# Rotary rotation moved from a product on TensorE to DMAs between partitions, with the index rope four attention units later

## The chip, the cores and the metric

One core of one Trainium2 chip runs the whole program as one launch. The metric is the device time of that launch in microseconds (us). Engines: TensorE (PE, with its weight loads as PEld), VectorE (DVE), ScalarE (ACT), GpSimd (POOL), and SyncE (SP), which issues the weight loads. Each engine works through its own list of instructions in order; semaphores tie the lists together.

## The reference, cut to what matters

A first block (a convolution mixer and a mixture of 32 experts) is followed by two layers of a second block. Only the second block is touched:

```python
def apply_rope(x, cos, sin):
    x1, x2 = jnp.split(x, 2, axis=-1)               # halves of a head's 64 channels
    return jnp.concatenate([x1 * c - x2 * s, x2 * c + x1 * s], axis=-1)

for l in range(DEPTH_2):                             # two layers
    (qa, ka, va, qb, kb, vb, qc, kc, vc, qi, ki, wi, gates) = split(rmsnorm(x) @ w_in[l])
    o_a = chunk_band_attention(qa, ka, va, rel_bias_a[l])
    o_b = diff_attention(apply_rope(qb), apply_rope(kb), vb, lam, lam_init, subln_b[l])
    o_c = dsa_attention(apply_rope(qc), apply_rope(kc), vc, apply_rope(qi), apply_rope(ki), wi, topk)
    ...                                              # gates, up, out, cross attention, swiglu
```

Everything is float32. Five tensors a layer go through `apply_rope`: qb, kb, the index pair (qi and ki together, called idx), qc and kc.

## The kernel before

Activations lie transposed: 128 channels on the partitions (two heads of 64), 256 tokens along a row. A tensor of heads is `[128, 4, 256]`, four blocks of 128 channels; idx has three blocks. A weight of 1024 x 128 is a "chunk". For each chunk ACT writes a rounded copy `w_hi` ("split", line 1292), DVE writes the rest `w_lo` ("low", line 529), and PE multiplies three times (lines 734, 735, 737). For the chunks of qc, kc and vc (35 to 46 of a layer) POOL does the low part, on the same line 529. Four chunk buffers (`PARTS`) go round, so ACT may split chunk n+4 only when PE has used chunk n.

The order of a layer is the hand-written list `WORK` (line 157); `with_splits` puts the splits and lows into it, and every engine walks through the result. `attention(first, last, extra)` lays out the attention units: at step s come "probs" of unit s-1, the extra work of the step, "scores" of unit s, "turn" (transposes) of unit s-1 and "apply" of unit s-2. Units 0 to 7 are attention A, with one chunk of gate projections as extra work at steps 1 to 8. At each unit DVE adds the bias and takes the row maximum (1730, 1731), ACT takes the exponential (1179), DVE divides by the sum (1737, 1745), PE transposes (1045), ACT copies the transposed probabilities out (`probsT`), PE applies them (1064), and ACT copies the result out (`outs`, which frees the unit's PSUM).

PSUM is four "duos" of 1024 columns. `seat` gives every tenant a duo and a turn: units go round duos 0 to 2, gate tenants g_0 to g_5 take duo 3, all others go round all four. `enter` waits until the tenant before in the same duo has been freed. Unit 5 sits where unit 2 sat.

A rope is: PE multiplies the heads by a constant matrix `rotate` of +1 and -1, which swaps the 32-partition halves of each head with a sign (line 996); DVE multiplies that product by `sin_r` (1698); POOL multiplies the heads by `cos_r` in place (1857); DVE adds the two (1703). The ropes of qb and kb stand behind the projections of kb and vb. The index rope stands at step 1 of attention A, behind "probs" 0. With it go the index weights: PE turns 64 rows of `score` into PSUM (1000), and DVE scales them into `wi` (1709), which frees the tenant p_idx. p_idx sits in duo 1 and the next tenant there is unit 1; g_0 follows vb in duo 3.

After attention A comes the index stage: two top-64 selections on DVE ("index" 0 and 1; products on line 1755, eight values at a time on 1760 and 1762, the selection on 1763), while PE runs the projections of qc, kc and vc and their two ropes. After it DVE does the rope of qc, the lows of chunks 47 to 49, the rope of kc and the scores of unit 8, in this order.

Of the kernel before, what the change touches and what calls it, by code (L numbers as in the profile page):

```python
# [13 lines left out]
ALU = mybir.AluOpType  # L14
# [30 lines left out]
LAYER_LINKS = 124  # L45
# [106 lines left out]
def gate_parts(starts, piece, gate):  # L152
# [7 lines left out]
        + attention(0, 8, {**gate_parts((1, 5), 7, 0), 1: [("rope", 2, "idx"), ("gates", 7, 0, 0)]})  # L160
# [74 lines left out]
def tenants(work):  # L235
    names = []
    for w in work:
# [5 lines left out]
        elif kind == "rope":  # L243
            names.append(f"r_{w[2]}")
# [43 lines left out]
def build(nc, x, mem, cst, vec1, vec2, relpad, w_in, w_out, w1, w3, w2, w_in_2, w_up_a, w_up_b, w_up_c,  # L288
# [11 lines left out]
    with ExitStack() as ctx:  # L300
        def sb(name, shape, dt=F32):
            return ctx.enter_context(nc.sbuf_tensor(name, shape, dt))
# [47 lines left out]
        rtok = sb("rtok", [P, 16])  # L350

# [69 lines left out]
        def small(*dims):  # L421
# [34 lines left out]
         lam_dot, lam_exp, rot_done, cos_ready, rope_ready, idx_raw, wi_turned, idx_done, relu_ready, selneg_ready,  # L456
# [10 lines left out]
            "lam_dot lam_exp rot_done cos_ready rope_ready idx_raw wi_turned idx_done relu_ready selneg_ready "  # L467
# [29 lines left out]
        def arrived(eng, i):  # L497
            eng.wait_ge(ring_full[MIX_SLOTS[i]], MIX_SLOTS[:i + 1].count(MIX_SLOTS[i]) * 16)

# [196 lines left out]
        def _(pe):  # L696
# [261 lines left out]
            for l in range(LAYERS):  # L958
                for w in WORK:
# [27 lines left out]
                    elif kind == "rope":  # L987
                        r, name = w[1], w[2]
                        if name == "idx":
                            pe.wait_ge(idx_raw, l + 1)  # L990
                        else:
                            freed(pe, f"p_{name}", l)
# [5 lines left out]
                        if name == "idx":  # L998
                            for t in range(TT):
                                last = pe.transpose(duo("p_idx")[:, 768 + 64 * t:832 + 64 * t],  # L1000
                                                    score[64:128, t * P:(t + 1) * P], ident[64:128, 64:128])
                            last.then_inc(wi_turned, 1)
# [172 lines left out]
        def _(act_e):  # L1175
# [107 lines left out]
            for l in range(LAYERS):  # L1283
                for w in WORK_SPLIT:
# [29 lines left out]
                    elif kind == "proj" and w[2] not in ("qa", "ka"):  # L1314
                        product_done(act_e, w[1], l)
                        name = w[2]
                        copy(heads[name], view(duo(f"p_{name}"), 0, 4, SEQ)).then_inc(free_of(f"p_{name}"), 1)
                    elif kind == "proj_v":
# [7 lines left out]
                    elif kind == "index_proj":  # L1326
# [4 lines left out]
                        copy(score[64:128, :], duo("p_idx")[64:128, 512:768]).then_inc(idx_raw, 1)  # L1331
                    elif kind == "gates":
# [69 lines left out]
        def _(v):  # L1402
# [29 lines left out]
            v.wait_ge(consts_in, 32)  # L1432
            norm("n_mix", 1, xT, g1("norm_mix"), hT)
# [202 lines left out]
            for l in range(LAYERS):  # L1636
                link, linked = linker(v, layer_chain, LAYER_LINKS, l)
                for w in WORK_SPLIT:
# [23 lines left out]
                    elif kind == "root":  # L1662
# [31 lines left out]
                    elif kind == "rope":  # L1694
                        r, name = w[1], w[2]
                        k = 3 if name == "idx" else 4
                        v.wait_ge(rot_done, l * 5 + r + 1)
# [8 lines left out]
                        if name == "idx":  # L1706
# [233 lines left out]
```

## Time and profile before

| | |
|---|---|
| time, median of 3 runs | 1865.93 us (1864.66 to 1867.06) |
| the profiled execution | 1867.45 us, its span 1865.7 us, so 1.75 us lie around the span |
| PE busy | 1673.9 us, 90% |
| DVE / ACT / POOL busy | 881.0 / 586.0 / 95.4 us |
| mean granted PE clock | 0.951 |
| first block, then two layers | layers from about 694 us to 1274 us and from there to 1851 us |

The trace gives for each instruction its start, its length, and, where its engine stood idle before it, how long and which instruction released it. A length contains time in which the instruction waited inside its engine. The second layer repeats the first 576.5 us later, to within a few hundredths of a us in the stretches used here (ACT's table load behind the idx copies starts at 787.85 and at 1364.35 us), so every reading is made in the first and counted twice.

### The profile page before, as it was taken

Reading aid. Unit: us, or ns where it says so; the run is one execution under the profiler, and the core shown is the slowest. Engines: PE = TensorE matmul, PEld = TensorE weight load, DVE = VectorE, ACT = ScalarE, POOL = GpSimd, SP = SyncE. Lnnn points to the kernel's source line nnn. Section 1 sums busy time; section 2 is a strip of 40 time slices with the busy share of each in tenths; the row PEclk is TensorE's granted clock in tenths of the full one; section 3 lists DMA queues with packets and bytes.
Section 4 is the critical chain, followed back from the end, with each engine's and each line's share of the span. In section 5 each row is a group of like instructions: output and inputs, shape, how many; then the busy total and the mean of one; then the engine's idle time right before and its main releaser. Section 6 shows DMA issues by size and latency. Waiting matters only on the chain.

```text
span 1865.7 us, 24506 instructions
## 1 busy us (share of the span) xinstructions
PE 1673.9 (90%) x10574; PEld 1335.2 (72%) x10574; DVE 881.0 (47%) x1157; ACT 586.0 (31%) x881; POOL 95.4 (5%) x50
## 2 busy tenths in 40 slices
PE   6948799999999969998999799998999799889997
PEld 5836544344443438877779689998978678779997
DVE  1782311111011136568745376646467755366653
ACT  1030211111111124453532344434454451244442
POOL 0000000000000000134000000000016000000000
PEclk8978799999999999999999799999999999979998
DMA  9052199999999974423323255473434224326550
GB/s 341 1 225 90 70 428 430 429 428 428 429 430 427 428 284 145 160 101 126 136 88 138 90 181 181 166 244 136 163 120 158 91 91 142 128 91 199 175 192 23
DMA packets 121739, 388.73 MB, mean 208 GB/s; under 512 B 3504, under 2 KB 55088, under 8 KB 109360
## 3 DMA queue, kind: packets, MB, share of 16 engines
q1 hardware_dynamic: 121648, 387.40, 54.1%
q8 instruction: 71, 1.16, 0.3%
q14 instruction: 20, 0.16, 0.0%
HBM read 386.34 MB, written 1.05 MB: 208 GB/s over the span
## 4 chain that ended last, share of the span: by engine, by line
PE 63%; DVE 17%; DMA 10%; ACT 6%; issue 2%; SPq 0%; DVEq 0%; ACTq 0%
DMA ring<-w 10%; PE psum L915 9%; PE psum L734 7%; PE psum L735 7%; PE psum L737 7%; PE psum L1092 4%; PE psum L724 4%; PE psum L937 3%; DVE outs L1452 3%; PE psum L766 3%; PE psum L1151 2%; PE psum L1154 2%; PE psum L1153 2%; ACT probs L1179 2%; DVE w_lo L529 2%
## 5 line engine op out<-in xcount | busy, mean ns | idle before, releaser
L529 DVE TENSOR_TENSOR w_lo<-raw,w_hi 128x1024 fp32r<-128x1024 f32 x250 | 305.8, 1240 | 196.0 <-ACT w_hi L1182 195.0
L1182 ACT ACTIVATE w_hi<-raw 128x1024 fp32r<-128x1024 f32 x274 | 284.4, 1053 | 282.8 <-PE psum L737 111.2
L734 PE MATMUL psum<-h_hi,w_hi 128*128 128x256 f32 x1456 | 364.2, 288 | 8.5 <-DVE big L1680 6.8
L735 PE MATMUL psum<-h_hi,w_lo 128*128 128x256 f32 x1456 | 358.8, 284 | 0.0
L734 PEld LDWEIGHTS psum<-h_hi,w_hi 128*128 128x128 f32 x1456 | 280.7, 193 | 14.9 <-DVE big L1680 8.5
L735 PEld LDWEIGHTS psum<-h_hi,w_lo 128*128 128x128 f32 x1456 | 280.8, 193 | 0.1
L915 PE MATMUL psum<-ring,outs 128*64 128x512 f32 x1024 | 231.5, 608 | 23.9 <-DMA ring<-w 22.5
L915 PEld LDWEIGHTS psum<-ring,outs 128*64 128x64 f32 x1024 | 81.3, 140 | 172.0 <-issue 172.0
L737 PE MATMUL psum<-h_lo,w_hi 128*128 128x256 f32 x1456 | 204.2, 283 | 0.0
L1613 DVE TENSOR_TENSOR qk<-big,psum 128x512 f32<-128x512 f32 x16 | 17.2, 1077 | 368.3 <-PE psum L915 368.3
L737 PEld LDWEIGHTS psum<-h_lo,w_hi 128*128 128x128 f32 x1456 | 187.8, 192 | 0.0
L1182 ACT ACTIVATE qk<-psum 128x1024 f32<-128x1024 f32 (+1 forms) x48 | 39.6, 829 | 343.1 <-PE psum L922 166.1
L937 PE MATMUL psum<-ring,qk 128*64 128x512 f32 x512 | 113.4, 595 | 0.0
L1151 PE MATMUL psum<-act_parts,w_hi 128*128 128x256 f32 x352 | 98.9, 281 | 0.0
L1153 PE MATMUL psum<-act_parts,w_hi 128*128 128x256 f32 x352 | 98.9, 281 | 0.0
L1154 PE MATMUL psum<-act_parts,w_lo 128*128 128x256 f32 x352 | 98.9, 281 | 0.0
L1179 ACT ACTIVATE probs<-probs,stat 128x256 f32<-128x256 f32 (+1 forms) x112 | 50.8, 454 | 123.3 <-DVE stat L1731 123.3
L1092 PE MATMUL psum<-outs,raw 128*128 128x256 f32 x384 | 83.2, 379 | 0.0
L937 PEld LDWEIGHTS psum<-ring,qk 128*64 128x64 f32 x512 | 35.3, 137 | 66.8 <-issue 66.8
L1857 POOL TENSOR_TENSOR qk<-qk,std 128x1024 f32<-128x1024 f32 x8 | 21.1, 2635 | 1189.2 <-PE psum L996 1189.2
L1092 PEld LDWEIGHTS psum<-outs,raw 128*128 128x128 f32 x384 | 73.0, 190 | 10.0
L724 PE MATMUL psum<-hT,ring 128*128 128x256 f32 x320 | 71.6, 388 | 7.1 <-DVE hT L1422 7.1
(230 smaller groups left out, 2238.8 us busy)
## 6 DMA issues: line engine op xcount, KB each, us to landing
ring<-w SPq DMA_DIRECT2D x96, 2048.0 KB, 16.7
raw<-w_in SPq DMA_DIRECT2D x30, 2048.0 KB, 7.6
raw<-w_gu SPq DMA_DIRECT2D x44, 1024.0 KB, 7.2
raw<-w_down SPq DMA_DIRECT2D x12, 1536.0 KB, 6.4
ring<-w_in SPq DMA_DIRECT2D x5, 2048.0 KB, 17.2
raw<-w_out SPq DMA_DIRECT2D x4, 2048.0 KB, 8.0
ring<-w_out SPq DMA_DIRECT2D x2, 2048.0 KB, 14.3
raw<-w_up_a SPq DMA_DIRECT2D x2, 2048.0 KB, 7.7
```

The costliest lines, as they stand in the source:

```text
L529: return eng.tensor_tensor(chunk_part(w_lo, n), chunk_raw(n), chunk_part(w_hi, n).bitcast(F32), ALU.subtract)
L724: last = mm(to[:, o, :], w[:, k, o * P:(o + 1) * P], rhs[:, k, :], start=(k == 0), stop=(k == k_chunks - 1))
L734: mm(to, hi[:, k, :], h_hi[:, k, :], start=(k == 0), stop=False)
L735: mm(to, lo[:, k, :], h_hi[:, k, :], start=False, stop=False)
L737: last = mm(to, hi[:, k, :], h_lo[:, k, :], start=False, stop=(k == KD - 1))
L915: last = mm(psum[rows, 1, bank * 512:bank * 512 + 512], xs[:, k, cols], view(ring[:, at + e, :], 0, KD, D_EXPERT)[:, k, :], start=(k == 0) ...
L937: last = mm(psum[rows, 2, half * 512:half * 512 + 512], hidT[:, f, rows], view(ring[:, 4 + e, :], 0, 4, D)[:, f, half * 512:half * 512 + 512],
L1092: last = mm(to[:, o, :], wu[:, k, oo * P:(oo + 1) * P], outs[:, b, k, :], start=(k == 0), stop=(k == 3))
L1151: mm(to, hi[:, o, :], act_hi[:, k, :], start=(k == 0 and o % 2 == 0), stop=False, skip_group_check=True)
L1153: mm(to, hi[:, o, :], act_lo[:, k, :], start=False, stop=False, skip_group_check=True)
L1154: last = mm(to, lo[:, o, :], act_hi[:, k, :], start=False, stop=(k == KF - 1), skip_group_check=True)
L1182: return nca.activation(out_ap, in_ap, ACT.Copy)
```

## The change

The matrix product is gone. Instead ACT, as soon as it has copied a tensor of heads out of PSUM, issues four DMAs from SBUF to SBUF, one for each group of 32 partitions, which write the heads with the halves swapped into one half of the scratch `sq` (the first for ropes 0, 2 and 4, the second for 1 and 3). A fifth operand carries the sign: `side`, a column of +1 and -1, is computed once at the start on DVE and multiplied into `sin_r`. DVE's first step now reads SBUF and writes in place, and POOL and DVE wait for the DMAs (`rotation_in`) instead of for PE. The five PSUM tenants r_* are gone, which moves all later tenants: p_idx now sits in duo 3, and the next tenant of duo 3 is g_0; i_0 follows unit 6 in duo 0, i_1 follows unit 7 in duo 1.

The index weights become work of their own at step 1, and the index rope moves to step 4, behind the last chunk of gate 0. In the finished list the split and the low of chunk 33, which stood behind scores 4 and probs 4, now stand ahead of the rope, so DVE's order there is: gate 0 (line 1680), low 33, index rope, scores 4. ACT's is: gate 0's tanh, split 33, exponential 4, turn 3, apply 2. POOL's is: gate 0 (line 1864), then the cosine part of the index rope. The DMAs of idx are still issued where its projection is copied out.

```diff
-        + attention(0, 8, {**gate_parts((1, 5), 7, 0), 1: [("rope", 2, "idx"), ("gates", 7, 0, 0)]})
+        + attention(0, 8, {**gate_parts((1, 5), 7, 0), 1: [("index_weights",), ("gates", 7, 0, 0)],
+                           4: [("gates", 7, 0, 3), ("rope", 2, "idx")]})
...
-        elif kind == "rope":
-            names.append(f"r_{w[2]}")
...
+        def rotated(r):
+            return sq[:, 4 * (r % 2):4 * (r % 2) + 4]
+
+        def rotate(eng, r, name, l):
+            k = 3 if name == "idx" else 4
+            if r >= 2:
+                eng.wait_ge(rope_ready, l * 5 + r - 1)
+            for at in range(0, P, 32):
+                eng.dma_start(rotated(r)[at:at + 32, 0:k, :], heads[name][at ^ 32:(at ^ 32) + 32, 0:k, :]
+                              ).then_inc(rot_odd if r % 2 else rot_even, 16)
...
-                        enter(pe, f"r_{name}", l)
-                        to = view(duo(f"r_{name}"), 0, 4, SEQ)
-                        for k in range(3 if name == "idx" else 4):
-                            last = mm(to[:, k, :], c("rotate"), heads[name][:, k, :], start=True, stop=True)
-                        last.then_inc(rot_done, 1)
...
                         copy(heads[name], view(duo(f"p_{name}"), 0, 4, SEQ)).then_inc(free_of(f"p_{name}"), 1)
+                        freed(act_e, f"p_{name}", l)
+                        rotate(act_e, ROPES.index(name), name, l)
...
                         copy(score[64:128, :], duo("p_idx")[64:128, 512:768]).then_inc(idx_raw, 1)
+                        act_e.wait_ge(idx_raw, l + 1)
+                        rotate(act_e, 2, "idx", l)
...
+            link(v.tensor_reduce(side[:], c("rotate"), AX.X, ALU.add))
...
-                            link(v.tensor_tensor(sin_r, c("sin"), rstd[:], ALU.mult))
+                            link(v.scalar_tensor_tensor(sin_r, c("sin"), side[:], rstd[:], ALU.mult, ALU.mult))
...
-                        v.tensor_tensor(sq[:, 0:k], view(duo(f"r_{name}"), 0, 4, SEQ)[:, 0:k],
-                                        sin_r.unsqueeze(1).broadcast_to([P, k, SEQ]), ALU.mult
-                                        ).then_inc(free_of(f"r_{name}"), 1)
-                        freed(v, f"r_{name}", l)
+                        rotation_in(v, r, l)
+                        part = rotated(r)[:, 0:k]
+                        link(v.tensor_tensor(part, part, sin_r.unsqueeze(1).broadcast_to([P, k, SEQ]), ALU.mult))
                         v.wait_ge(cos_ready, l * 5 + r + 1)
-                        v.tensor_tensor(heads[name][:, 0:k], heads[name][:, 0:k], sq[:, 0:k], ALU.add
+                        v.tensor_tensor(heads[name][:, 0:k], heads[name][:, 0:k], part, ALU.subtract
                                         ).then_inc(rope_ready, 1)
...
-                        pool.wait_ge(rot_done, l * 5 + r + 1)
+                        rotation_in(pool, r, l)
```

## Rows read from the trace of the kernel before

**Rows 1.** The page's chain of work that ended last, by engine

```profile
PE 63%; DVE 17%; DMA 10%; ACT 6%; issue 2%; SPq 0%; DVEq 0%; ACTq 0%
```

**Rows 2.** That chain from 700 to 960 us: start, us, what

```profile
763.14 1.73 PE psum L996 x8
...
869.42 3.54 DVE w_lo L529 x2
...
877.54 0.43 DVE probs L1730
```

**Rows 3.** Timeline of ACT: start, us, engine, line, operation [idle before <- releaser]

```profile
751.66 1.03 ACT L1182 ACTIVATE qk<-psum 128x1024 f32<-128x1024 f32 x1 [1.82 <-PE psum L737]
...
787.85 1.28 ACT L1179 ACT_TABLE_LOAD   x1
```

**Rows 4.** Timeline of DVE at the first two units of attention A

```profile
790.26 1.39 DVE L1745 TENSOR_TENSOR probs<-probs,stat 128x256 f32<-128x256 f32 x1
791.57 0.94 DVE L1698 TENSOR_TENSOR sq<-psum,v 128x768 f32<-128x768 f32 x1
...
793.54 0.35 DVE L1709 TENSOR_SCALAR wi<-psum,rtok 128x4 f32<-128x4 f32 x2
```

**Rows 5.** Timeline of PE there: gate chunk 27 begins, scores of unit 1

```profile
789.64 0.39 PE L734 MATMUL psum<-h_hi,w_hi 128*128 128x256 f32 x1
...
793.95 0.70 PE L1035 MATMUL psum<-qk 64*128 64x256 f32 x4 [1.18 <-DVE wi L1709]
```

**Rows 6.** Timeline of DVE at step 4: scores of unit 4

```profile
809.35 0.41 DVE L1730 SCALAR_TENSOR_TENSOR probs<-psum,win 128x256 f32<-128x256 f32 x1
```

**Rows 7.** Timeline of ACT at step 4: tanh of gate 0, copy of apply 2

```profile
809.47 1.06 ACT L1179 ACTIVATE big<-big 128x1024 f32<-128x1024 f32 x1 [2.00 <-DVE big L1680]
...
812.63 0.26 ACT L1182 ACTIVATE outs<-psum 128x128 f32<-128x128 f32 x1
```

**Rows 8.** Timeline of PE at step 5: scores of unit 5

```profile
812.94 0.70 PE L1035 MATMUL psum<-qk 64*128 64x256 f32 x4 [0.32 <-ACT outs L1182]
```

**Rows 9.** Timeline of POOL from the index rope to the end of the index stage

```profile
789.53 1.84 POOL L1857 TENSOR_TENSOR qiT<-qiT,std 128x768 f32<-128x768 f32 x1 [9.52 <-PE psum L996]
...
810.73 1.05 POOL L1864 TENSOR_SCALAR big<-big 128x1024 f32<-128x1024 f32 x1 [19.36 <-ACT big L1179]
...
831.84 9.67 POOL L529 TENSOR_TENSOR w_lo<-raw,w_hi 128x1024 fp32r<-128x1024 f32 x4 [1.42 <-ACT w_hi L1182]
...
845.77 7.26 POOL L529 TENSOR_TENSOR w_lo<-raw,w_hi 128x1024 fp32r<-128x1024 f32 x3 [1.38 <-ACT w_hi L1182]
853.50 2.57 POOL L529 TENSOR_TENSOR w_lo<-raw,w_hi 128x1024 fp32r<-128x1024 f32 x1 [0.47 <-ACT w_hi L1182]
...
869.58 3.32 POOL L1857 TENSOR_TENSOR qk<-qk,std 128x1024 f32<-128x1024 f32 x1 [7.87 <-PE psum L996]
```

**Rows 10.** Timeline of DVE in the index stage: products of index 0 and 1

```profile
834.43 7.23 DVE L1755 SCALAR_TENSOR_TENSOR score<-probs,wi,score 128x128 f32<-128x128 f32 x3
...
853.35 3.53 DVE L1755 SCALAR_TENSOR_TENSOR score<-win,wi,score 128x256 f32<-128x256 f32 x3
```

**Rows 11.** SP's DMA issues (ns min/median/max) and us to landing, by size

```profile
L688 SPq DMA_DIRECT2D raw<-w_in x32: 367/368/3506, 666.9 to 1461.8; - x32
...
ring<-w SPq DMA_DIRECT2D x96, 2048.0 KB, 16.7
...
consts<-cst SPq DMA_DIRECT2D x1, 64.0 KB, 1.9
```

**Rows 12.** Busy time in stretches of 1 us, PE first; PEclk after POOL

```profile
874.00:875.00 1.00, 0.53 (x4) 0.13 (x4) 1.00 (x1) 0.00 (x0) 0.00 (x0) 1.00 0.00 0
...
876.00:877.00 1.00, 0.00 (x0) 0.00 (x0) 0.97 (x2) 0.00 (x0) 0.00 (x0) 0.72 0.00 0
...
880.00:881.00 1.00, 0.51 (x3) 0.52 (x4) 0.96 (x3) 0.00 (x0) 0.00 (x0) 0.50 0.00 0
...
883.00:884.00 1.00, 1.00 (x9) 1.00 (x9) 0.90 (x4) 0.99 (x2) 0.00 (x0) 0.87 0.00 0
```

More of the change, by code:

```diff
@@ L44 @@
 NEG = -1.0e30
-LAYER_LINKS = 124
+LAYER_LINKS = 129
 TAKEN = -3.0e38
@@ L350, in build @@
         rtok = sb("rtok", [P, 16])
+        side = sb("side", [P, 1])
         def c(name):
@@ L466, in build @@
             "w2_done ysb_ready scat_done scat_added moe_chain "
-            "lam_dot lam_exp rot_done cos_ready rope_ready idx_raw wi_turned idx_done relu_ready selneg_ready "
+            "lam_dot lam_exp rot_even rot_odd cos_ready rope_ready idx_raw wi_turned idx_done relu_ready selneg_ready "
             "scores_done rowmax_ready exp_ready probs_ready probsT_done probsT_ready attn_done subln_ready "
@@ L498, in arrived, with rotation_in @@
             eng.wait_ge(ring_full[MIX_SLOTS[i]], MIX_SLOTS[:i + 1].count(MIX_SLOTS[i]) * 16)
+        def rotated(r):
[7 more added lines that the diff above has]
+                              ).then_inc(rot_odd if r % 2 else rot_even, 16)
+        def rotation_in(eng, r, l):
+            if r % 2:
+                eng.wait_ge(rot_odd, (l * 2 + r // 2 + 1) * 64)
+            else:
+                eng.wait_ge(rot_even, (l * 3 + r // 2 + 1) * 64)
         def raw_of(i):
@@ L986, in _ @@
                             split_chunk(w[1], o, duo("p_idx")[:, o * SEQ:(o + 1) * SEQ], l)
[L987 to L992, printed above, removed]
-                        enter(pe, f"r_{name}", l)
-                        to = view(duo(f"r_{name}"), 0, 4, SEQ)
-                        for k in range(3 if name == "idx" else 4):
-                            last = mm(to[:, k, :], c("rotate"), heads[name][:, k, :], start=True, stop=True)
-                        last.then_inc(rot_done, 1)
[L998 to L1002, printed above, removed]
+                    elif kind == "index_weights":
+                        pe.wait_ge(idx_raw, l + 1)
+                        for t in range(TT):
+                            last = pe.transpose(duo("p_idx")[:, 768 + 64 * t:832 + 64 * t],
+                                                score[64:128, t * P:(t + 1) * P], ident[64:128, 64:128])
+                        last.then_inc(wi_turned, 1)
                     elif kind == "index":
@@ L1696, in _ @@
                         k = 3 if name == "idx" else 4
-                        v.wait_ge(rot_done, l * 5 + r + 1)
-                        v.tensor_tensor(sq[:, 0:k], view(duo(f"r_{name}"), 0, 4, SEQ)[:, 0:k],
-                                        sin_r.unsqueeze(1).broadcast_to([P, k, SEQ]), ALU.mult
-                                        ).then_inc(free_of(f"r_{name}"), 1)
-                        freed(v, f"r_{name}", l)
+                        rotation_in(v, r, l)
+                        part = rotated(r)[:, 0:k]
+                        link(v.tensor_tensor(part, part, sin_r.unsqueeze(1).broadcast_to([P, k, SEQ]), ALU.mult))
                         v.wait_ge(cos_ready, l * 5 + r + 1)
-                        v.tensor_tensor(heads[name][:, 0:k], heads[name][:, 0:k], sq[:, 0:k], ALU.add
+                        v.tensor_tensor(heads[name][:, 0:k], heads[name][:, 0:k], part, ALU.subtract
                                         ).then_inc(rope_ready, 1)
                         v.wait_ge(rope_ready, l * 5 + r + 1)
-                        if name == "idx":
-                            v.wait_ge(wi_turned, l + 1)
-                            for t in range(TT):
-                                last = v.tensor_scalar(wi[:, t, :], duo("p_idx")[:, 768 + 64 * t:772 + 64 * t],
-                                                       tok_mix[:, t:t + 1], 0.5, ALU.mult, ALU.mult)
-                            last.then_inc(free_of("p_idx"), 1)
+                    elif kind == "index_weights":
+                        v.wait_ge(wi_turned, l + 1)
+                        for t in range(TT):
+                            last = v.tensor_scalar(wi[:, t, :], duo("p_idx")[:, 768 + 64 * t:772 + 64 * t],
+                                                   tok_mix[:, t:t + 1], 0.5, ALU.mult, ALU.mult)
+                        last.then_inc(free_of("p_idx"), 1)
                     elif kind == "scores":
```

2 lines of the change are left out of this document (1 added, 1 removed).

## Prediction, made before any run of the change

> **What bounds the kernel now.** I read the page's chain first: PE holds 63% of what ended last, DVE 17% [rows 1]. I then took the same chain for one layer, because what a rope is worth differs by stage. Three stages matter. In the projections PE never stops: the products of the qb rope are themselves links of the chain [rows 2], and ACT stands idle 1.82 us before its copy [rows 3]. In attention A the chain passes between PE, ACT and DVE at every unit, and a delay of any one is passed on. In the index stage the chain is DVE alone, from the selection through the ropes of qc and kc to scores 8 at 877.54 [rows 2]; PE's ropes of qc and kc are hidden there. All terms below are for one layer and count twice. The sum is made on the profiled run (1867.45 us, its span and 1.75 around it), which lies 1.5 us above the median of 1865.93; I give times as median plus change.
>
> **Part A, the products leave PE.** Ropes of qb and kb: 1.73 us each on the chain [rows 2] (kb's, the same again, starts at 775.80). Two of them: -3.5 us. The cover for what replaces them: four issues on ACT and a transfer. No row shows a DMA issued by ACT. Nearest is SP's, 0.37 us each, the longest 3.5 us [rows 11]; I take 0.37, so 1.5 us for four, between 0 and 14 us. ACT has 1.82 us of idle at each chunk [rows 3], and the buffers let it run up to three chunks ahead, so 1.5 us is hidden. The transfer of 512 KB has rows on both sides: 1.9 us for 64 KB alone and 16.7 us for 2 MB in a full queue [rows 11]. I take 2 to 5 us because it is near the small one. qb is copied by 752.7 [rows 3], and DVE comes to its rope shortly before PE ends kb's projection at 763.14 [rows 2]; that is some 10 us of room for 1.5 + 5 and POOL's cosine step of 2.4. Cost nothing, unless the transfer is late (rival 2). The first step of a rope on DVE, now from SBUF, keeps its length unless POOL blocks it (part C). The column `side` (once, at the start, while DVE waits for its first norm) and the changed `sin_r` product lie beside PE work: 0.
>
> **Part B, index weights at step 1.** Before, ACT went from the idx copies into the exponential's table load at 787.85 [rows 3], DVE divided at 790.26, and then came two rope steps and `wi` at 793.54 [rows 4]. PE did gate chunk 27 meanwhile and waited only 1.18 us for `wi` before scores 1 at 793.95 [rows 5]. Now ACT issues four DMAs ahead of the table load: everything behind it, probs 0 among it, moves by 1.5. The division starts at 791.74. Its 1.39 us held a wait for POOL's cosine step, which ended at 789.53 + 1.84 = 791.37 [rows 4, 9]; that step is elsewhere now, and I take 0.42, as of the equal shape in [rows 6]. `wi` then ends at 792.6. The gain is undone by the seats: p_idx is now ahead of g_0 in duo 3, so PE can't begin chunk 27 before `wi`. It begins at 792.6 instead of 789.64 [rows 5], takes its 3.1 us, and scores 1 starts at 795.8 instead of 793.95: +1.85. Bounds: with issues that cost nothing +0.35, with issues of 1 us +4.4.
>
> **Part C, index rope at step 4.** This is the dear one. Before, DVE did scores 4 at 809.35, right behind gate 0 [rows 6]. Queued ahead of it now: low 33, which needs split 33, which stands behind the tanh of 809.47 on ACT [rows 7]. A copy of that size is another 1.05, so low 33 can start at 811.5 and ends at 812.7. Then two rope steps of 0.95 each. POOL's cosine step (1.84) can't start before its gate step ends at 811.8 [rows 9]. DVE's first rope step now has both inputs in SBUF. Where two-input steps of DVE met POOL, each took one whole turn of POOL: three products in 7.23 us beside POOL's four in 9.67, 2.41 against 2.42 apiece [rows 9, 10]. So I let them take turns: low 33 to 812.7, POOL to 814.5, rope steps to 816.4, scores 4 at 816.4 instead of 809.35: 7.05 later.
> Who waits: ACT's exponential 4, and queued behind it on ACT turn 3 and apply 2, whose copy at 812.63 freed the PSUM of unit 2 [rows 7]. PE's scores 5 waited for just that copy [rows 8]. From scores 4 to that copy: 0.85 on DVE, 0.85 for the exponential, 0.5 and 0.25 for the copies, about 2.55 with hand-offs. PE's scores 5 starts at 819.0 instead of 812.94 [rows 8]: +6.0. Lower bound, if POOL and DVE run side by side: the cosine step is then done at 813.65 together with DVE's first step, scores 4 comes at 814.6, PE's scores 5 at 817.15, +4.2. Low 33 is done early for it, but DVE's low there was no link of the chain, so this returns nothing. Upper bound +6.5.
>
> **Part D, the clock.** PE now stands idle about 4.3 us at step 1 and 6 us at step 5. The rows show what that does: PE stops in the middle of 874 to 875, the granted clock is 0.72 in 876 to 877 and 0.50 after, PE starts again in the middle of 880, and only in 883 to 884 does the clock return to 2.4 GHz from 1.2 [rows 12]. Some 2.6 us of PE work at the lower level cost about 1.2. Two such idles: +2.4 (0 to +3).
>
> **Part E, index stage.** DVE's way out gets shorter: POOL's cosine step of kc (869.58, 3.32 us) no longer falls between the lows. The three lows took 5.7 us from 869.42 (two of them 3.54, [rows 2, 9]) and would take 3.5: -2.1. Against it: the four issues for qc hold up ACT's split 42 and with it POOL's low of 845.77 [rows 9] by 1.5 us. That closes POOL's gaps, the one ahead of 853.50 among them. DVE's last three products of index 1 took 3.53 because they slipped through those gaps [rows 10]; in lock step with POOL they take 7.2, +3.7, and start 0.95 earlier: +2.75. So -2.1 + 2.75 = +0.65. DVE still passes rope qc, three lows, rope kc. A shorter idle of PE ahead of unit 8 may save the 1.2 of part D, so I take 0, from -2.5 to +1.
>
> **Sum.** -3.5 + 1.85 + 6.0 + 2.4 + 0 = +6.75 a layer, +13.5 for two: 1865.9 + 13.5 = 1879.4.
>
> **Against the Trainium skill.** Rows first: 1.39 us for a division that needs 0.42 while POOL worked, and products that kept step with POOL [rows 4, 9, 10]. The Trainium skill (SBUF — State Buffer, Who interferes with whom) says that a VectorE instruction with two SBUF inputs and a GpSimd instruction that reads SBUF exclude each other for a whole instruction, and that one input from PSUM avoids this. The trace agrees. By that rule this change puts one more step of every rope among those that can be blocked; without it part C would be 4.2.
> The Trainium skill (DMA: Bandwidth & Descriptors, Rules for kernel authors) advises one large transfer over several for parts of the partitions, since all share the same 16 engines. No row here shows a transfer from SBUF to SBUF. By it the four transfers would go one behind the other, which changes nothing in the sum as long as they land within 5 us.
>
> **Rivals.**
> 1. *Not slower: the stalls are short.* If an issue on ACT costs next to nothing, the POOL gaps stay, DVE is not held by POOL at step 4, and the clock holds: -3.5 + 0.35 + 4.2 + 0 - 2.1 = -1.05, twice: 1863.8. With 0.37 for an issue and the rest the same it is +0.45: 1866.8. It decides at the point where scores 4 is later by less than about 4 us. Against it: split 33 alone puts 2.1 us of waiting into DVE's queue. For it: ACT's issue cost is not in the trace. Chance 0.17.
> 2. *The transfers are late.* Near 17 us [rows 11], qb's rotation lands at 771 and POOL is done at 773.5; DVE stands at that rope, and low 23 behind it is wanted by PE three chunks of vb (2.73 us each: from 764.87 to 775.80 for four) after 763.14, at 771.3; with its own 1.2 us and the rope's last step that is +3.3 to +4.6, of which I take 3.3. kc's lands at 875, so its rope ends some 1.6 later. +4.9 a layer above my sum: 1889. Against it: 16.7 is the row of a queue that never emptied, and a load of 64 KB took 1.9. Chance 0.10.
> 3. *The lock does not bite at step 4*, POOL and DVE overlapping: part C 4.2, 1875.8. Chance 0.18.
> 4. *Issues on ACT are dear*, 1 us each: part B +4.4, and 2.5 more in the index stage: +11.8 a layer, 1889.5. Chance 0.10.
> My forecast has the rest, 0.45.
>
> **How the numbers follow.** The likeliest case is 1879.4; with part D from 0 to 3, part E from -2.5 to +1 and part C up to 6.5 its own range is 1870 to 1884. With rival 3 and parts of 1, 2 and 4 the range is 1866 to 1890; about 1 in 10 is left below, 1 in 10 above. A measurement of this kernel can tell about 0.2% (3.7 us) from no change. Faster than 1862.2 only in the far half of rival 1: 0.05. Within 0.2%: 0.13. Slower: 0.82.
>
> **What would show it.** Right: no products of line 996; at step 5 PE waits 5 to 6 us for ACT's copy of apply 2; before gate chunk 27 PE waits about 4 us for `wi`; the clock at 0.50 after both; scores 8 on DVE about as far behind the second product of index 0 as before (834.43 to 877.54, 43.1 us). DMA issues on ACT of 0.37. Wrong: if PE's wait at step 5 is under 3 us, part C fails; if DVE is found waiting for a rotation, rival 2 holds; if the index stage shrinks by over 2 us, part E was too dark.

## The result, and the profile after

Measured: 1881.73 us, the median of five runs (1878.98 to 1887.96), beside 1866.90 us for the kernel before (1864.66 to 1868.28): 1.0088 times as long, 95% interval 1.0063 to 1.0114. The forecast was 1879.4 us, slower. The profiled execution took 1879.01 us, its span 1877.2; the stages below are read from it.

The products on PE are gone, and PE's busy time fell by only 5.2 us (1668.7 after 1673.9): what is left of PE's work ran more often at 1.2 GHz. From the page of the changed kernel, PE's line of busy time, the mean clock and the two DMA rows that are new (line 510, issued by ACT; size and median us to landing):

```profile
PE 1668.7 (89%) x10498; PEld 1330.5 (71%) x10498; DVE 883.2 (47%) x1158; ACT 585.9 (31%) x881; POOL 100.3 (5%) x50
...
q10 hardware_dynamic: 1920, 4.98, 1.2%
...
sq<-qk ACTq DMA_DIRECT2D x32, 128.0 KB, 2.4
```

```profile
core 0: 1877.2 us, clock 0.943
```

The stretches of a layer, each from the start of one instruction to the start of another, the changed kernel less the kernel before, first and second layer:

| stretch | change, us | forecast |
|---|---|---|
| copy of qb to copies of idx (projections) | -3.48 / -3.48 | -3.5 |
| copies of idx to scores 1 on DVE (step 1) | +4.56 / +4.83 | +1.85, and 1.2 for the clock |
| scores 1 to scores 5 (step 4) | +6.40 / +6.40 | +6.0 |
| scores 5 to the first product of index 0 | +2.24 / +2.34 | +1.2 for the clock |
| that product to scores 8 (index stage) | -3.67 / -3.57 | 0 |
| sum | +6.05 / +6.52 | +6.75 |

Outside these stretches the profiled pair differs too: the first copy of qb came 2.6 us earlier with the changed kernel, in work that the two kernels share, and the work behind scores 8 took 0.5 and 1.0 us longer. So the two spans lie 11.5 us apart, the medians 14.8.

**Step 1.** Timeline of ACT in the changed kernel; it answers to [rows 3]:

```profile
780.11 1.25 ACT L1192 ACTIVATE qiT<-psum 128x512 f32<-128x512 f32 x3 [1.82 <-PE psum L757]
781.36 0.38 ACT L1192 ACTIVATE score<-psum 64x256 f32<-64x256 f32 x1
781.77 2.44 ACTq L510 DMA_DIRECT2D sq<-qiT  x4
784.25 1.28 ACT L1189 ACT_TABLE_LOAD   x1 [2.50 <-issue]
```

The four issues take 2.44 us, 0.61 each, and the table load comes 4.14 us after the first idx copy, where it came 1.65 after (786.20 and 787.85). Then DVE and PE, which answer to [rows 4, 5]:

```profile
786.65 0.42 DVE L1758 TENSOR_TENSOR probs<-probs,stat 128x256 f32<-128x256 f32 x1
787.00 0.34 DVE L1722 TENSOR_SCALAR wi<-psum,rtok 128x4 f32<-128x4 f32 x2
793.17 0.69 DVE L1743 SCALAR_TENSOR_TENSOR probs<-psum,win 128x512 f32<-128x512 f32 x1 [5.83 <-PE psum L1045]
```

```profile
787.39 0.58 PE L754 MATMUL psum<-h_hi,w_hi 128*128 128x256 f32 x1 [5.26 <-DVE wi L1722]
787.77 0.41 PE L755 MATMUL psum<-h_hi,w_lo 128*128 128x256 f32 x1
```

The division is down to 0.42 us. Gate chunk 27 stands behind `wi` and starts 7.28 us after the idx copy (3.44 before); its products take 0.41 us, against 0.28 at the full clock, and scores 1 on PE comes 5.0 us behind its start.

**Step 4.** DVE, POOL and, at step 5, PE; they answer to [rows 6, 9, 8]:

```profile
809.96 1.34 DVE L549 TENSOR_TENSOR w_lo<-raw,w_hi 128x1024 fp32r<-128x1024 f32 x1 [2.07 <-ACT w_hi L1192]
811.23 2.55 DVE L1714 TENSOR_TENSOR sq<-sq,v 128x768 f32<-128x768 f32 x1
813.81 0.96 DVE L1716 TENSOR_TENSOR qiT<-qiT,sq 128x768 f32<-128x768 f32 x1
814.80 0.42 DVE L1743 SCALAR_TENSOR_TENSOR probs<-psum,win 128x256 f32<-128x256 f32 x1
```

```profile
810.20 2.77 POOL L1870 TENSOR_TENSOR qiT<-qiT,std 128x768 f32<-128x768 f32 x1
```

```profile
817.29 1.22 PE L1045 MATMUL psum<-qk 64*128 64x256 f32 x4 [6.21 <-ACT outs L1192]
```

Low 33 waits 2.07 us for split 33, the first rope step is held by POOL's cosine step (2.55 us in place of 0.95), and scores 4 is 6.98 us later against scores 1 than before. PE waits 6.21 us for ACT's copy.

**The clock behind it.** One us a line; PEclk is the granted clock, third from the right:

```profile
816.00:817.00 1.00, 0.00 (x0) 0.00 (x0) 0.34 (x2) 1.00 (x6) 0.00 (x0) 0.50 0.00 0
821.00:822.00 1.00, 1.00 (x7) 1.00 (x7) 0.83 (x2) 1.00 (x4) 0.00 (x0) 0.50 0.00 0
822.00:823.00 1.00, 1.00 (x8) 1.00 (x8) 0.94 (x2) 0.47 (x3) 0.00 (x0) 0.71 0.00 0
823.00:824.00 1.00, 1.00 (x11) 1.00 (x10) 0.30 (x1) 0.00 (x0) 0.00 (x0) 1.00 0.00 0
```

PE works again from 817.29 and does so at 1.2 GHz for 5.3 us, to 822.6.

**Index stage.** PE's sixteen index products, ACT's copy behind them ("relu 1", ahead of split 38), POOL, then DVE; the last two answer to [rows 9, 10]:

```profile
837.38 2.66 PE L1022 MATMUL psum<-qiT 64*128 64x128 f32 x16
```

```profile
840.10 1.03 ACT L1189 ACTIVATE win<-psum 128x1024 f32<-128x1024 f32 x1 [0.84 <-PE psum L1022]
```

```profile
838.91 2.37 POOL L549 TENSOR_TENSOR w_lo<-raw,w_hi 128x1024 fp32r<-128x1024 f32 x1 [1.89 <-ACT w_hi L1192]
842.24 4.83 POOL L549 TENSOR_TENSOR w_lo<-raw,w_hi 128x1024 fp32r<-128x1024 f32 x2 [0.96 <-ACT w_hi L1192]
...
856.58 9.51 POOL L549 TENSOR_TENSOR w_lo<-raw,w_hi 128x1024 fp32r<-128x1024 f32 x4 [4.02 <-ACT w_hi L1192]
866.04 2.48 POOL L1870 TENSOR_TENSOR qk<-qk,std 128x1024 f32<-128x1024 f32 x1
```

```profile
841.47 3.32 DVE L1768 SCALAR_TENSOR_TENSOR score<-probs,wi,score 128x128 f32<-128x128 f32 x3
...
853.62 1.53 DVE L1768 SCALAR_TENSOR_TENSOR score<-win,wi,score 128x256 f32<-128x256 f32 x3
...
866.27 3.33 DVE L1714 TENSOR_TENSOR sq<-sq,v 128x1024 f32<-128x1024 f32 x1
869.63 3.29 DVE L1716 TENSOR_TENSOR qk<-qk,sq 128x1024 f32<-128x1024 f32 x1
```

POOL has an idle of 0.96 us where it had none, and the three products of index 0 take 3.32 us in place of 7.23. POOL's next long idle, ahead of the low of chunk 42, is 4.02 us in place of 1.38; the four products of index 1 (from 853.10) fall into it and take 2.0 us together in place of 6.1. These two make up most of the gain: the last selection comes 8.85 us earlier against the first product. Then POOL works from 856.6 to 875.2 without a pause, DVE's rope of qc takes 6.6 us beside it in place of 2.5, and scores 8 is only 3.67 us earlier.

### The profile page after: what moved, and what is told of

It reads as the page before. It is cut to its first block, busy times and chain, and to the rows that moved or that the text cites. A ratio compares the mean times of both kernels' runs of the same rounds, so it can differ in the third digit from the quotient of the medians.

```text
span 1877.2 us, 24389 instructions
## 1 busy us (share of the span) xinstructions
PE 1668.7 (89%) x10498; PEld 1330.5 (71%) x10498; DVE 883.2 (47%) x1158; ACT 585.9 (31%) x881; POOL 100.3 (5%) x50
## 4 chain that ended last, share of the span: by engine, by line
PE 63%; DVE 17%; DMA 10%; ACT 6%; issue 2%; ACTq 0%; SPq 0%; DVEq 0%
DMA ring<-w 10%; PE psum L935 9%; PE psum L754 7%; PE psum L755 7%; PE psum L757 7%; PE psum L1102 4%; PE psum L744 4%; PE psum L957 3%; PE psum L786 3%; DVE outs L1467 3%; PE psum L1164 2%; PE psum L1161 2%; PE psum L1163 2%; DVE w_lo L549 2%; ACT probs L1189 2%
## 5 line engine op out<-in xcount | busy, mean ns | idle before, releaser
L549 DVE TENSOR_TENSOR w_lo<-raw,w_hi 128x1024 fp32r<-128x1024 f32 x250 | 313.9, 1276 | 200.4 <-ACT w_hi L1192 199.4
L754 PE MATMUL psum<-h_hi,w_hi 128*128 128x256 f32 x1456 | 369.3, 290 | 19.4 <-DVE wi L1722 10.5
L755 PE MATMUL psum<-h_hi,w_lo 128*128 128x256 f32 x1456 | 364.1, 287 | 0.0
L754 PEld LDWEIGHTS psum<-h_hi,w_hi 128*128 128x128 f32 x1456 | 284.8, 196 | 26.6 <-DVE wi L1722 10.8
L755 PEld LDWEIGHTS psum<-h_hi,w_lo 128*128 128x128 f32 x1456 | 285.1, 196 | 0.2
```

The costliest lines, as they stand in the source:

```text
L549: return eng.tensor_tensor(chunk_part(w_lo, n), chunk_raw(n), chunk_part(w_hi, n).bitcast(F32), ALU.subtract)
L754: mm(to, hi[:, k, :], h_hi[:, k, :], start=(k == 0), stop=False)
L755: mm(to, lo[:, k, :], h_hi[:, k, :], start=False, stop=False)
```

## The experiments

Four questions: what each half of the change costs alone, what of the dear steps can be undone, why the index stage became shorter, and whether the parts can be put together so that they pay. Pairs of numbers such as -3.48 / -3.48 give the change of a stretch against the kernel before, first and second layer, as in the table above; stretches are read from one profiled execution of each kernel.

**The rotation by DMA alone**, the index rope where it was:

```diff
-1: [("index_weights",), ("gates", 7, 0, 0)], 4: [("gates", 7, 0, 3), ("rope", 2, "idx")]
+1: [("index_weights",), ("rope", 2, "idx"), ("gates", 7, 0, 0)]
```

> The changed kernel with the index rope back at step 1, right behind the index weights; the rotation by DMA and all else as changed. Theory (the place at step 4 is the dear part: 6.4 us a layer at step 4 and 2.3 us of lower clock behind it): both go, the index rope hides behind gate chunk 27, so about 17 us less than the changed kernel, 1864 us, give or take 7 for what the index stage does. Rival (the cost lies in the DMAs and their issue on ACT): stays within 4 us of the changed kernel, about 1880. In the trace the wait of PE's scores 5 for ACT's copy is 0.3 us by the theory, 6 by the rival.

Measured 1867.18 us, 1.0005 of the kernel before (0.9996 to 1.0015). Projections -3.48 / -3.48, step 1 +5.06 / +5.26, scores 1 to scores 5 0, index stage -3.13 / -1.80. So the projections pay what was forecast, step 1 takes back more than that, and all of step 4's loss belongs to the move.

**The move alone**, the rotation still a product on PE (which sits in duo 3, between gates 0 and 1; p_idx keeps its place in duo 1):

```diff
-1: [("rope", 2, "idx"), ("gates", 7, 0, 0)]
+1: [("index_weights",), ("gates", 7, 0, 0)], 4: [("gates", 7, 0, 3), ("rope", 2, "idx")]
```

> The kernel before with only the place changed: rotation still a product on PE, index weights at step 1, index rope at step 4 (its product sits in duo 3 between gates 0 and 1). Theory: step 4 costs 6 to 8 us a layer and the clock 1 to 2 more, step 1 gives back 1 to 2, so 10 to 16 us more than before, 1877 to 1883. Rival (the DMAs are the cost): within 3 us of the kernel before.

Measured 1870.26 us, 1.0022 (1.0013 to 1.0032), some 7 us below the range that I expected. Step 1 returns 2.74 us in both layers, since the two rope steps and the wait for the cosine step are gone from it; scores 1 to scores 5 costs 5.51 / 5.16, and the second layer's index stage is 2.88 us shorter. DVE at step 4, with the rotation in PSUM:

```profile
808.01 0.94 DVE L1701 TENSOR_TENSOR sq<-psum,v 128x768 f32<-128x768 f32 x1
809.87 0.96 DVE L1706 TENSOR_TENSOR qiT<-qiT,sq 128x768 f32<-128x768 f32 x1 [0.91 <-POOL qiT L1860]
```

The first step is no longer held, but the second waits 0.91 us for the cosine step: scores 4 is 6.26 us later against scores 1, where it is 6.98 with both inputs in SBUF, so the input from PSUM saves 0.7 us there.

**The index weights back in duo 1**, so that gate chunk 27 need not wait for `wi`:

```diff
-            d, others = others % DUOS, others + 1
+            d, others = {"p_idx": 1}.get(name, others % DUOS), others + 1
```

> The changed kernel with one tenant moved: the index projection sits in duo 1 again, so gate chunk 27 no longer follows it and unit 1 does. Theory (PE's wait of 5.3 us ahead of chunk 27 comes from the seat): chunk 27 starts behind the turn of the index weights, scores 1 waits for wi instead, 5 us a layer less, with the clock at full rate there: 10 us less in all, 1872. Rival (PE waits for ACT's issues wherever the tenant sits): under 3 us less in all.

Measured 1875.19 us, 1.0047 (1.0030 to 1.0064). Copies of idx to scores 1 is -0.46 / -0.47 in place of +4.56 / +4.83: the place in PSUM alone is worth 5.0 to 5.3 us a layer at this point. The whole is 6.5 us less than the changed kernel, not 10: in the first layer 1.0 us comes back before scores 5 (+7.40), and the index stage differs between the two layers, -3.49 and +2.25, which is taken up below.

**The index rope at step 7**, where DVE has idle time. With it the order of splits and lows goes back to that of the kernel before, so low 33 leaves its place ahead of scores 4 too (the lines below are of the first of the two):

```diff
-4: [("gates", 7, 0, 3), ("rope", 2, "idx")]
+7: [("gates", 8, 1, 2), ("rope", 2, "idx")]
```

> The changed kernel with the index rope at step 7 instead of 4, behind gate 1's third chunk, where DVE stood idle about 2 us, and with splits and lows left in the order of the kernel before. Theory (what counts at step 4 is what DVE has queued ahead of scores 4: low 33 and the rope, 7 us together): the wait at step 5 falls from 6.2 to 0.3 us, the clock stays up, step 7 loses at most 1 us: 15 us less than the changed kernel, 1866. Rival (the rope costs the same wherever it stands in attention A): within 4 us of the changed kernel.

Measured 1872.42 us, 1.0033 (1.0021 to 1.0046). Step 4 costs nothing (rope and low 33 are both gone from it, so this run doesn't price them apart), step 7 costs 3.93 / 3.93, for a reason that I hadn't seen: POOL's cosine step stands behind a low of POOL's own, and DVE waits between its two rope steps. DVE and POOL of that kernel:

```profile
825.00 0.96 DVE L1716 TENSOR_TENSOR qiT<-qiT,sq 128x768 f32<-128x768 f32 x1 [4.12 <-POOL qiT L1870]
```

```profile
820.48 2.61 POOL L549 TENSOR_TENSOR w_lo<-raw,w_hi 128x1024 fp32r<-128x1024 f32 x1 [9.49 <-ACT w_hi L1192]
823.06 1.83 POOL L1870 TENSOR_TENSOR qiT<-qiT,std 128x768 f32<-128x768 f32 x1
```

**The cosine step early**, in POOL's list at step 1, DVE's steps still at step 4:

```diff
-                    elif kind == "rope":
+                    elif kind == "index_weights" or (kind == "rope" and w[2] != "idx"):
```

> The changed kernel, with one thing moved: the cosine step of idx is done by POOL right before it would have been done in the kernel before (at step 1, beside the index weights), not at step 4. DVE's two rope steps and low 33 stay ahead of scores 4. Theory (the lock between the two engines costs part of step 4): DVE's first rope step, 2.55 us long in the trace of after because POOL's cosine step began 1 us before it, falls to 0.96, so scores 4 and PE's scores 5 come 1.6 us earlier in each layer; step 1 may give back 0 to 1 us, because DVE's division meets the cosine step there; 3 us in all, near 1878. Rival (the length of that step is not POOL's doing): the step stays above 2 us, and the time that of the changed kernel.

Measured 1880.58 us, 1.0071 (1.0056 to 1.0087). Scores 1 to scores 4 is 20.06 us in place of 21.63, and the row shows why:

```profile
813.37 0.94 DVE L1714 TENSOR_TENSOR sq<-sq,v 128x768 f32<-128x768 f32 x1
814.35 0.96 DVE L1716 TENSOR_TENSOR qiT<-qiT,sq 128x768 f32<-128x768 f32 x1
```

So 1.6 us of step 4 were POOL's hold on DVE, as forecast; step 1 gave 0.3 to 0.5 back. The total of 3 us can't be told from none between sets of runs of this spread. What the two engines do here is what the Trainium skill (SBUF — State Buffer, Who interferes with whom) says of two SBUF inputs beside a GpSimd read; 2.55 against 0.94 us for the same step is this case's number for it.

**The issues behind exponential 0**, not ahead of its table load:

```diff
+                        if u == 0:
+                            act_e.wait_ge(idx_raw, l + 1)
+                            rotate(act_e, 2, "idx", l)
```

> The changed kernel, with one thing moved: ACT issues the four transfers of idx's rotation behind exponential 0, not ahead of the exponential's table load. Theory (four issues at 2.4 us stand between the idx copies and the division): table load, division, index weights and PE's gate chunk 27 come 2.4 us earlier, so from the idx copy to scores 1 the change is +2.2 us in place of +4.6; step 4 stays at +6.4 since the transfers are needed only there. 5 us in all, near 1876; 1 to 2 us more if PE's shorter idle spares it the low clock. Rival (PE's wait at step 1 is set by something other than the issues, the seat alone): PE's wait for the index weights stays at 5.3 us and nothing is gained, or the 2.4 us come back at step 2, where ACT's turn 0 then stands behind the issues: near 1881.

At the place itself it did what was expected: step 1 +2.16 / +1.60 in place of +4.56 / +4.83, and PE waits 2.78 us for `wi`, not 5.26. The whole did not follow: 1882.58 us, 1.0082 (1.0067 to 1.0098), where I had expected 1876. Two readings of the one execution that has a trace say where it went there. The first layer began 5.5 us later than in the profile of the changed kernel, in work that the two kernels share. And the index stage of the second layer took 48.3 us in place of 41.7. The miss is that I priced an edit in a kernel whose index stage has two lengths.

**Why the index stage became shorter: the places in PSUM?** My first theory: i_1 now shares a duo with unit 7, so relu 1, and with it split 38, come late.

```diff
+PLACE = {'i_0': 3, 'i_1': 0, 'p_qc': 1, 'p_kc': 2, 'p_vc': 3}
```

> The changed kernel, with only the places in PSUM of the index stage set back to those of the kernel before (i_0, i_1, and the projections qc, kc, vc); the index weights keep their new place. Two theories for the 8.9 us that the products of the index stage lose in the trace of after. Seats: i_1 now shares its place with unit 7, relu 1 and with it split 38 come late, POOL stands idle and DVE's products run at 3.3 us for three in place of 7.2: with the old places the first product group of index 0 takes about 7.2 again and the stretch from the first product to the selection is some 4 us longer than in the changed kernel, while the later part, in which POOL blocks the rope of qc, gives part of it back; total 0 to +4 us. Issues: the 2.4 us of transfer issues on ACT delay the splits, whatever the seats: the first product group stays near 3.3 us and the stretch stays at -9.

1881.16 us, 1.0075 (1.0060 to 1.0091); in the first layer first product to selection 25.45 us (25.44 in the changed kernel), products 3.33 us. The seats have no part in it, and that theory fell.

Set side by side, the eighteen index stages of the nine kernels so far show what goes with what. PE's sixteen index products took either 1.58 to 1.68 us or 2.66 to 2.93 us, and these are the two clocks.

| rotation | index products on PE | stages | products 2 to 4 of index 0 on DVE | first product to scores 8 |
|---|---|---|---|---|
| product on PE | 1.58 us | 3 | 7.2 us | 45.2 |
| product on PE | 2.93 | 1 (the move alone, second layer) | 1.13 | 42.4 |
| by DMA | 2.66 to 2.93 | 12 | 1.13 to 3.36 | 41.6 to 43.4 |
| by DMA | 1.68 | 2 | 7.34 | 47.5 and 48.3 |

One row of each kind from the second layer of the kernel with the late issues (PE, POOL, DVE):

```profile
1420.69 1.68 PE L1022 MATMUL psum<-qiT 64*128 64x128 f32 x16
```

```profile
1422.22 9.78 POOL L549 TENSOR_TENSOR w_lo<-raw,w_hi 128x1024 fp32r<-128x1024 f32 x4 [1.42 <-ACT w_hi L1192]
```

```profile
1424.82 7.34 DVE L1769 SCALAR_TENSOR_TENSOR score<-probs,wi,score 128x128 f32<-128x128 f32 x3
```

That is a coincidence in rows, not yet a cause. The chain that it suggests: PE at 1.2 GHz is late with the index products, so ACT is late with relu 1 (it waits 0.84 us for PE in the row above) and the splits behind it, POOL stands still for 1 us, and in that pause DVE's products get ahead of POOL's next low. The test makes the pause without touching PE.

**The kernel before, with one useless copy more**, 1.06 us on ACT ahead of relu 1:

```diff
+                        if t == 1:
+                            copy(sq[:, 0:4], heads["qb"])
```

> The kernel before, with one copy more on ACT (128 x 1024, about 1 us, into scratch that nobody reads) between relu 0 and relu 1 of the index stage; it adds work and removes none. Theory for the index stage: where relu 1, and behind it split 38, comes 1 us late, POOL stands idle for 1 us after its low of chunk 37, and DVE's products of index 0, which otherwise take turns with POOL (7.23 us for three), slip through in 1.1 to 3.4 us. So: POOL's first idle 0.7 to 1.2 us, the three products at most 3.4 us, from the first product to the selection 25 to 28 us in place of 34.3, to scores 8 42 to 43 in place of 45.2, and the whole kernel 5 to 6 us faster than before, near 1861. Rival (PE's lower clock itself, or the ropes by transfer, shortens the stage, and POOL's gap goes with it by chance): the products stay at 7.2 us and the kernel takes 1 to 2 us longer than before.

Measured 1861.89 us, 0.9976 (0.9967 to 0.9986): work was added and the kernel became 4.6 us faster. Its second layer, with PE at 2.4 GHz (PE, ACT, POOL, DVE):

```profile
1401.98 1.58 PE L1012 MATMUL psum<-qiT 64*128 64x128 f32 x16
```

```profile
1403.70 1.06 ACT L1182 ACTIVATE sq<-qk 128x1024 f32<-128x1024 f32 x1
1404.65 1.02 ACT L1179 ACTIVATE win<-psum 128x1024 f32<-128x1024 f32 x1
```

```profile
1403.51 2.41 POOL L529 TENSOR_TENSOR w_lo<-raw,w_hi 128x1024 fp32r<-128x1024 f32 x1 [1.42 <-ACT w_hi L1182]
1406.80 9.55 POOL L529 TENSOR_TENSOR w_lo<-raw,w_hi 128x1024 fp32r<-128x1024 f32 x4 [0.88 <-ACT w_hi L1182]
```

```profile
1406.10 3.26 DVE L1757 SCALAR_TENSOR_TENSOR score<-probs,wi,score 128x128 f32<-128x128 f32 x3
```

In this layer POOL pauses 0.88 us, the products take 3.26 us in place of 7.22 (two of them 0.35 us each in the pause, the third 2.50, held by POOL's next low), and first product to scores 8 is 42.6 / 41.2 us in place of 45.2. In the second layer PE ran at its full clock, so the pause does it; neither the clock nor the ropes by DMA are needed for it. In the first layer the gain to scores 8 was 2.7 us, in the second 4.0.

**Split 38 ahead of relu 1**, in the changed kernel, to close the pause:

```diff
+AT = WORK_SPLIT.index(("index", 1))
+WORK_SPLIT[AT:AT + 2] = WORK_SPLIT[AT + 1], WORK_SPLIT[AT]
```

> The changed kernel, with one exchange in ACT's list: split 38 stands ahead of relu 1, not behind it. No work is added or removed. Theory: split 38 no longer waits for the index product on PE, so POOL's gap closes whatever PE's clock is; the three products of index 0 take 7.2 us again, the stretch from the first product to scores 8 becomes 45 to 48 us in place of 41.6, and the time is 7 to 13 us longer than that of the changed kernel, 1888 to 1894. Rival (the gap has another cause, for instance the lower clock of PE in the projection of qc): products at 1.1 to 3.4 us and a time within 2 us of the changed kernel's.

1879.68 us, 1.0081 (1.0065 to 1.0098); first product to scores 8 41.55 us in both layers: my expectation fell. POOL did its lows of 37 and 38 without a pause, and stood still 0.75 us one low later, waiting for split 39, which waited for PE at its low clock:

```profile
839.33 4.79 POOL L551 TENSOR_TENSOR w_lo<-raw,w_hi 128x1024 fp32r<-128x1024 f32 x2 [1.89 <-ACT w_hi L1194]
844.87 2.44 POOL L551 TENSOR_TENSOR w_lo<-raw,w_hi 128x1024 fp32r<-128x1024 f32 x1 [0.75 <-ACT w_hi L1194]
```

The products still took 3.15 us. The pause need not stand where I had put it; any one early in the products will do. Relu 1 is one way to it, a slow PE at the chunks of qc another.

**All four mends together**: the index rope at step 7 (with the order of splits and lows as there), its cosine step at step 1, its issues behind exponential 0 and no longer behind the idx copies, p_idx in duo 1.

```diff
-4: [("gates", 7, 0, 3), ("rope", 2, "idx")]
+7: [("gates", 8, 1, 2), ("rope", 2, "idx")]
-                    elif kind == "rope":
+                    elif kind == "index_weights" or (kind == "rope" and w[2] != "idx"):
+                        if u == 0:
+                            act_e.wait_ge(idx_raw, l + 1)
+                            rotate(act_e, 2, "idx", l)
+            d, others = {"p_idx": 1}.get(name, others % DUOS), others + 1
```

> All four mends together: index rope at step 7, where the queue of DVE has room, its cosine step done by POOL at step 1, its transfers issued behind exponential 0, and the index weights' product in a place of its own (duo 1). If the costs found singly add up, for each layer: -3.5 for the products gone from PE, -0.5 - 2.4 at step 1 (the seat returned 5.0 us of 4.6, the issues 2.4), 0 at step 7 (3.9 us there was a wait for POOL's cosine step, which is now long done), and the index stage between -3.5 and +2.2, by where POOL's queue stands. Sum -4 to -10, twice: 1847 to 1859, faster than the kernel before. Rival (the gain in attention A is taken back at the next wait, ACT's or POOL's): scores 1 early by 6 us, but unit 7 only by 3 or less, and the time 1860 to 1866.

1851.84 us (1851.40 to 1853.44), 0.9921 of the kernel before (0.9908 to 0.9935): it beats the kernel before by 16 us and the changed kernel (1881.73, of another set of runs) by some 30. Per layer: projections -3.48 / -3.48, step 1 -2.74 / -2.74, scores 1 to scores 7 +1.98 / +1.98, index stage -3.46 / -2.14. At step 7 the cosine step is long done, but DVE's second rope step meets POOL's low 35 and takes 3.00 us, which is the 2 us left there:

```profile
812.23 0.95 DVE L1718 TENSOR_TENSOR sq<-sq,v 128x768 f32<-128x768 f32 x1
813.21 3.00 DVE L1720 TENSOR_TENSOR qiT<-qiT,sq 128x768 f32<-128x768 f32 x1
```

**And the transfers of qc and kc issued behind splits 42 and 46**, on top of it:

```diff
+                        if n in (42, 46):
+                            name = "qc" if n == 42 else "kc"
+                            freed(act_e, f"p_{name}", l)
+                            rotate(act_e, ROPES.index(name), name, l)
```

> The kernel with all four mends, and one thing more: ACT issues the transfers of qc behind split 42 and those of kc behind split 46, not ahead of them. Theory (the 2.45 us of issues hold split 42 back, so POOL's four lows of 9.5 us start 2.5 us late and its cosine steps end late, and DVE's rope of qc behind them is blocked): POOL's idle of 4.04 us ahead of those lows falls below 2.5, POOL is done some 2 us earlier, scores 8 comes 1 to 2.5 us earlier in each layer, 1847 to 1850. Rival (DVE is held by taking turns with POOL as such, whenever POOL starts; or the earlier lows close a gap in which the products of index 1 run): 0 to +4 us, 1852 to 1856.

1852.88 us (1849.38 to 1854.59), 0.9926 (0.9912 to 0.9940): the same as without it. In the stage the theory holds: POOL's idle ahead of the low of chunk 42 is 1.38 us in place of 4.04, and first product to scores 8 is 40.3 / 41.1 us in place of 41.8 / 43.1. The mechanism named under the rival shows as well: without the long pause the four products of index 1 take 6.1 / 6.2 us, where they took 2.0 with it. The last three of them:

```profile
840.33 3.74 DVE L1778 SCALAR_TENSOR_TENSOR score<-win,wi,score 128x256 f32<-128x256 f32 x3
```

So the issues on ACT cost on DVE's way out and give part of it back in the products; both together cost 1.5 / 2.0 us in the stage. The profiled execution was 2.5 us shorter (span 1847.6 against 1850.1), which the medians do not show. Whether it pays stays open.

## Why the prediction was right

The sum of +6.75 us a layer stands against +6.05 and +6.52, and the whole of +13.5 against 14.8 in the medians and 11.5 in the profiled pair. It is right in sign and in the size of the whole, and its two largest terms, A and C, are right by mechanism and size. Three others missed, and that they nearly cancel is luck.

**Part A held.** -3.5 us forecast, -3.48 in both layers. The transfers landed in 2.1 to 3.8 us, and no rope step of DVE waited for one, in the projections or elsewhere: rival 2 is out.

**Part B: the mechanism held, the issue was mis-sized.** The path over the division, `wi` and gate chunk 27 is in the rows. I had taken 0.37 us for an issue from SP's row [rows 11]; on ACT it is 0.61, so 2.44 us stand where 1.5 stood. Rival 4 had the cause, though at 1 us. The experiment with the late issues gets 2.4 and 3.2 us back at this point, the one with the seat 5.0 and 5.3.

**Part C held.** Scores 4 was to be 7.05 us later and is 6.98; scores 5 on PE was to be 6.0 later, and is 5.9 later against scores 1 on PE (24.88 us from one to the other, 18.99 before). The lock did bite: rival 3 is out, and the early cosine step prices it at 1.6 us.

**Part D was too small.** I had taken 1.2 us for an idle from [rows 12], where PE came back and had the full clock 2.8 us later (I had read 2.6). Here it stayed at 1.2 GHz for 4.5 us after the idle of step 1 (787.39 to 791.85; 5.1 in the second layer) and 5.3 us after that of step 5 (5.7). Step 1 lost about 1.9 us by it (chunk 27 to scores 1 took 5.0 us, 3.1 of it work at the full clock), and from scores 5 on it was 2.2 to 2.3, with 0.5 more in scores 5 itself. Both idles together cost 4.6 to 4.7 us, not 2.4. Why the clock came back later here than in [rows 12] stays open.

**Part E failed, by -3.6 us.** I had ACT's issues hold up split 42 and so close POOL's pauses ahead of the products of index 1, for +2.75. They do hold it up, but what comes of it here is a pause, 4.02 us where it was 1.38, and those products run in it: -4.0 us. That DVE is there in time is the work of a smaller pause twelve us earlier, 1 us in POOL's row at split 38, opened by PE's low clock at the index products, which I hadn't looked for: another -3.9. Nor did DVE's way out get 2.1 us shorter. It became 5.2 us longer, since its rope of qc (6.6 us in place of 2.5) now meets POOL's work, and POOL's cosine step of kc (871.80, 3.39 us) still falls on the lows, which took 5.58 us where I had 3.5 (3.50 in the last kernel above, whose issues stand behind split 42). My own mark was "if the index stage shrinks by over 2 us, part E was too dark", and it did. Where PE was at 2.4 GHz at the index products and the first pause was missing, in two stages, POOL's long pause was there as well (4.1 and 4.9 us), but DVE came too late for it: the four products of index 1 took 10.0 us, in lock step with POOL as part E had it, and the stage with the ropes by DMA was 2.3 and 3.1 us longer than before. The error was to hold that the stage stays in the pattern in which the trace of before shows it.

**Rival 1** (not slower) needed both stalls short; neither was. What kept the sum near the forecast is that some 3.1 us too little in parts B and D met 3.6 us too much in part E.

Not settled: which kernel's runs meet which clock at the index products. The five runs of the changed kernel fall in two groups (1878.98 to 1881.73, and 1887.73 and 1887.96), as one or two long index stages would make them, but only one of them, of the lower group, has a trace.

## What to carry to other kernels

Price a DMA by what its issuing engine does next: here no rope step of DVE waited for a transfer, while four issues, 2.4 us on ACT, were on the path at two places of a layer (step 1, and ahead of split 42). Before moving a step to another place, list for each engine what stands directly ahead of it and behind it there, and what frees the PSUM place that its product sits in; one place was worth 5 us, and a cosine step queued behind a low cost 4. Where two engines take turns, as DVE and POOL do here, look for the pauses of the one, since a 1 us pause let three products of the other shrink by 4 to 6 us, and in the kernel with nothing but that pause added 2.7 and 4.0 us of it reached the next stage; a stall, or even added work, can then be a gain.

## What the runs showed of the hardware

- An issue of a 128 KB or 96 KB transfer from SBUF to SBUF on ACT's queue took 0.61 us in the median (0.51 to 1.51, 40 issues of the changed kernel); SP's took 0.37 [rows 11]. ACT's arithmetic that stands ahead of them in its list went on beside them (exponential at 783.31, issue at 783.37, in the kernel with all mends). The Trainium skill (Perfetto Trace Analysis, DMA Instruction — HWDGE (DVE, Sync)) says that a DMA instruction keeps the issuing engine's sequencer until its descriptors are made; the 2.50 us of `issue` ahead of the table load agree.
- Such transfers, issued in fours, landed in 2.1 to 3.8 us each in the changed kernel, median 2.4.
- DVE's products with two SBUF inputs, once POOL paused for 0.9 to 1.2 us, ran there at 0.35 us each: all three behind the first in 1.13 us where the pause was 1.1 us or longer, two of three where it was 0.9 to 1.0, and only the third then waited for a whole low.
- PE, back from an idle of 5.3 and 6.2 us in the changed kernel, worked 4.5 to 5.7 us at 1.2 GHz; in [rows 12], back from 6.0, it did so for 2.8.
